# Neighbourhood attention two heads at a time, and a weight cast moved from GpSimd to ScalarE, in a three-layer kernel

## The chip, the cores and the metric

The kernel runs on one core of one Trainium2 chip. The metric is the device time of one execution in microseconds. Three runs of the kernel before gave 7265.52, 7279.33 and 7285.22, median 7279.33.

## The reference

Three layers follow one another on 2048 tokens of width 1024 with 256 context tokens. The first mixes pooling and two linear recurrences, the second a convolution and dense attention, the third a Fourier mixing and neighbourhood attention. Each has a projection in front, a gate and an output projection behind. The change touches the projection of the second layer and the neighbourhood attention of the third. In the latter the tokens form a grid of 32 rows of 64, there are 8 heads of 64, and a query sees 8 rows by 16 columns around it with a bias, and all context tokens, under one softmax:

```python
s_win = einsum('brqhd,brkwhd->bhrqkw', qg, kb) * scale + bias   # 8 rows of keys, masked to 16 columns
s_ctx = einsum('brqhd,bchd->bhrqc', qg, kc) * scale
p = softmax(concatenate([s_win, s_ctx]))
o = einsum('bhrqkw,brkwhd->brqhd', p_win, vb) + einsum('bhrqc,bchd->brqhd', p_ctx, vc)
```

## The kernel before, in words

The program is a row of stages; each stage's engines run their own lists, tied by semaphores, with a barrier between stages.

**The projection (`norm_project`, stage `p2`).** After a norm the input stands transposed in SBUF as a high and a low part (`hT`). The weights come in 22 columns of 128 (`w_sb`, two buffers). Each column is split into a high part (a cast, `split_high`, L146) and a low part (a subtraction, `split_low`, L151), both on GpSimd (L460 to L471). GpSimd may start on column n when TensorE has finished column n-2. TensorE waits for `w_split` and does for each of five token chunks (four of 512 and the context's 256) eight times three matmuls (L157 to L159). In this stage alone (`conv` is given) VectorE does the depthwise convolution of finished columns beside it: eight groups, each a few preparing instructions and then 31 taps, one SCALAR_TENSOR_TENSOR for each tap and run of tokens (L520; 60 or 90 behind one another). SyncE loads the groups' data in its own list between weight loads: group 3, for instance, in the place of column 8, behind the wait for the low part of column 6. ScalarE copies TensorE's chunks out and stores them.

**The neighbourhood attention (`neighbours`).** A first part builds the tables of biases. Then each of 8 heads goes through 16 steps of 128 queries (two grid rows). The window of a step has 9 grid rows of keys (576), the first two and last two steps have 8 (512). The 64 channels of a head are padded with zeros to 128 rows. For a step TensorE makes the scores (`win`, L2699 to L2702), VectorE adds the biases (L2772, L2775), takes the maxima (L2778 to L2780), ScalarE takes the exponentials with their sums (L2821, L2823), TensorE turns the weights by seven transposes (L2721), VectorE and ScalarE copy them to SBUF (`pt`), TensorE multiplies them with the values as the moving side (L2732), VectorE divides by the sum (L2789), TensorE turns the result (L2709), ScalarE copies it to `y`. There are two sets of score banks, and TensorE makes the scores three steps ahead. At the start of each head its values are turned (18 transposes) before the first step.

Of the kernel before, what the change touches and what calls it, by code (L numbers as in the profile page):

```python
# [161 lines left out]
def norm_project(nc, name, x_lat, x_ctx, mod, gain, w, out, groups, ident, eps, later=(), conv=None):  # L162
# [9 lines left out]
    with ExitStack() as ctx:  # L172
# [246 lines left out]
        with nc.Block() as block:  # L419
# [42 lines left out]
            def _(pool):  # L462
                for n in range(0 if later else 1, M):
# [5 lines left out]
                    split_high(nc.gpsimd, w_part[n % 2][0][:], w_sb[n % 2][:]).then_inc(w_high, 1)  # L469
# [63 lines left out]
            def _(act):  # L533
# [2031 lines left out]
def neighbours(nc, QKV, rpb, one_hot, ident, yT, row0):  # L2565
# [8 lines left out]
    VG = [range(0, 6), range(6, 12), range(12, 18)]  # L2574
    NGRP = len(VG) + 2 * QT + 1
# [7 lines left out]
    with ExitStack() as ctx:  # L2583
# [55 lines left out]

        q, k = [s.sb(f"q{u}", [P, SEQ]) for u in range(2)], [s.sb(f"k{u}", [P, T]) for u in range(2)]  # L2640
        vt = [s.sb(f"vt{u}", [HD, T]) for u in range(2)]
        v = s.sb("v", [P, NV, HD])
        NKEY = (R + 1) * ROW
        sw = [s.sb(f"sw{u}", [P, NKEY]) for u in range(2)]
        pr = [s.sb(f"p{u}", [P, NKEY + CTX]) for u in range(2)]
        pt = [s.sb(f"pt{u}", [P, 7, P]) for u in range(2)]
        mx = [s.sb(f"mx{u}", [P, 2]) for u in range(2)]
        nb = [s.sb(f"nb{u}", [P, 1]) for u in range(2)]
        sm = [s.sb(f"sm{u}", [P, 2]) for u in range(4)]
        rs = [s.sb(f"rs{u}", [P, 1]) for u in range(2)]  # L2650
        top_ = s.sb("top", [P, 1])
        o = [s.sb(f"o{u}", [P, HD]) for u in range(2)]
        y = [s.sb(f"y{u}", [HD, SEQ]) for u in range(2)]
        win = s.banks(4)
        tb = [ctx.enter_context(nc.psum_tensor(f"na_tb{u}", [P, NT], F32)) for u in range(2)]
        ob = ctx.enter_context(nc.psum_tensor("na_ob", [P, NT], F32))
        chain, zeroed = s.sem("chain"), s.sem("zeroed")
        in_full, in_used = s.sems("in_full", 2), s.sems("in_used", 2)
        s_full, s_free = s.sems("s_full", 2), s.sems("s_free", 2)
        t_full, t_free = s.sems("t_full", 2), s.sems("t_free", 2)  # L2660
        nb_ready, p_ready, pt_ready, v_ready = s.sem("nb_ready"), s.sem("p_ready"), s.sems("pt_ready", 2), s.sem("v_ready")
        o_full, o_norm, ot_out = s.sem("o_full"), s.sem("o_norm"), s.sem("ot_out")
        y_out, turn_ = s.sems("y_out", 2), s.sem("turn")

        def tiles(j):

            lo, rows, _, _ = window(j)
            n = rows * ROW
            a = [(i * P, min(P, n - i * P), lo * ROW // P + i) for i in range(-(-n // P))]
            return a + [(n + i * P, P, SEQ // P + i) for i in range(2)]  # L2670

        def heads(eng, body):
            with eng.Fori(0, NH // 2) as i:
                for u in range(2):
                    body(i * 2 + u, i, u)

        def grp(h, g):
            return g % 2, h * (NGRP // 2) + g // 2

        with nc.Block() as block:  # L2680
            @block.sync
            def _(sp):
                def body(h, pair, u):
                    sp.wait_ge(in_used[u], pair)
                    sp.dma_start(q[u][0:HD, :], QKV[ds(h * HD, HD), 0:SEQ]).then_inc(in_full[u], 16)
                    sp.dma_start(k[u][0:HD, :], QKV[ds(h * HD + NH * HD, HD), :]).then_inc(in_full[u], 16)
                    sp.dma_start(vt[u][:], QKV[ds(h * HD + 2 * NH * HD, HD), :]).then_inc(in_full[u], 16)
# [361 lines left out]
```

## Time and profile before

| | us |
|---|---|
| median of three runs | 7279.33 |
| the profiled execution | 7282.06 |
| its span | 7280.4 |
| busy in the span: TensorE matmul, weight load | 5664.7, 4331.2 |
| VectorE, ScalarE, GpSimd | 3688.1, 1714.0, 2075.9 |
| second projection, first to last matmul | 3574 to 4234 |
| attention loop, first score to last output | 6444 to 7072 |

Times in rows are counted from the span's start. The clock is the granted share of 2.4 GHz. Matmuls overlap, so a TensorE row's busy time includes the drain of its last one; the distance between starts is what it occupies.

### The profile page before, as it was taken

The numbers are of one execution on the slowest core, as the hardware profiler recorded it, in microseconds if no ns is written. First come the engines' busy times: TensorE is split into PE (matmuls) and PEld (weight loads), VectorE is DVE, ScalarE is ACT, GpSimd is POOL, SyncE is SP. The second block draws the span as 40 slices with busy tenths as digits, with TensorE's granted clock in tenths as the row PEclk, the third lists the DMA queues.
The fourth block names the chain that finished last, engine by engine and source line by source line (L and its number), as shares of the span: only waits on it lengthen the run. The fifth ranks groups of instructions, "written<-read, shape, count | busy, mean of one in ns | idle before, by whom it ended". The sixth has DMA issues, their size and how long they took to land. (4 is left out here: it accounts for less than half of the span.)

```text
span 7280.4 us, 117918 instructions
## 1 busy us (share of the span) xinstructions
PE 5664.7 (78%) x49713; PEld 4331.2 (59%) x49713; DVE 3688.1 (51%) x5261; ACT 1714.0 (24%) x3014; POOL 2075.9 (29%) x1372
## 2 busy tenths in 40 slices
PE   6899971139999556749586854999986999779989
PEld 1588850028888445627475732555574887357767
DVE  2100026654444666748499235888855000256667
ACT  2100002123332322213310021444413000124442
POOL 2211100024453312203467300766734111000002
PEclk8899985569999778879698986999996999879899
DMA  6312113332111111036322122000063211121115
GB/s 206 103 66 73 68 65 119 115 101 65 56 56 47 51 45 51 10 132 206 94 95 77 65 107 72 17 18 16 15 204 105 75 66 68 62 67 26 26 57 176
DMA packets 395963, 572.21 MB, mean 79 GB/s; under 512 B 62982, under 2 KB 296070, under 8 KB 375806
## 3 DMA queue, kind: packets, MB, share of 16 engines
q1 hardware_dynamic: 351126, 394.12, 17.4%
q10 hardware_dynamic: 33576, 127.83, 4.4%
q0 software_dynamic: 10752, 42.89, 2.1%
q8 instruction: 390, 6.39, 0.4%
q14 instruction: 119, 0.97, 0.0%
HBM read 360.86 MB, written 203.90 MB: 78 GB/s over the span
## 5 line engine op out<-in xcount | busy, mean ns | idle before, releaser
L157 PE MATMUL p_bank<-p_hT_high,p_w_high 128*128 128x512 f32 (+1 forms) x2928 | 1105.3, 377 | 139.4 <-POOL p_w_low L151 121.5
L158 PE MATMUL p_bank<-p_hT_low,p_w_high 128*128 128x512 f32 (+1 forms) x2928 | 1103.7, 377 | 0.0
L159 PE MATMUL p_bank<-p_hT_high,p_w_low 128*128 128x512 f32 (+1 forms) x2928 | 1102.7, 377 | 0.0
L491 DVE COPY p_o<-p_bank 128x512 f32<-128x512 f32 (+1 forms) x142 | 90.7, 639 | 1256.5 <-PE p_bank L159 1256.5
L146 POOL CAST p_w_high<-p_w 128x1024 fp32r<-128x1024 f32 x79 | 334.4, 4233 | 1345.7 <-issue 1152.6
L157 PEld LDWEIGHTS p_bank<-p_hT_high,p_w_high 128*128 128x128 f32 x2928 | 555.9, 190 | 242.1 <-POOL p_w_low L151 122.8
L158 PEld LDWEIGHTS p_bank<-p_hT_low,p_w_high 128*128 128x128 f32 x2928 | 555.7, 190 | 99.9
L159 PEld LDWEIGHTS p_bank<-p_hT_high,p_w_low 128*128 128x128 f32 x2928 | 555.1, 190 | 100.3
L2334 POOL TENSOR_TENSOR at_acc<-at_acc,at_p 128x512 f32<-128x512 f32 x256 | 426.4, 1665 | 142.2 <-ACT at_p L2272 120.5
L2376 DVE TENSOR_REDUCE at_mx<-at_mb 128x2 f32<-128x1024 f32 (+1 forms) x292 | 356.9, 1222 | 107.7 <-PE at_mb L2175 105.9
L1197 PE MATMUL rsc_db<-rsc_W,rsc_TK 64*64 64x64 f32 x8640 | 382.6, 219 | 4.6 <-issue 3.8
L2272 ACT ACTIVATE at_p<-at_sc 128x1024 f32<-128x1024 f32 (+1 forms) x296 | 284.9, 1013 | 400.3 <-PE at_sc L2164 348.4
L520 DVE SCALAR_TENSOR_TENSOR p_cy<-p_cu,p_wt,p_cy 128x512 f32<-128x512 f32 (+1 forms) x600 | 372.5, 700 | 0.0
L491 ACT COPY p_o<-p_bank 128x512 f32<-128x512 f32 x114 | 67.0, 588 | 1281.2 <-PE p_bank L159 1281.2
L157 PE MATMUL o_bank<-o_w_high,o_m_high 128*128 128x512 f32 x800 | 314.6, 393 | 66.9 <-POOL o_m_low L151 66.9
L1197 PEld LDWEIGHTS rsc_db<-rsc_W,rsc_TK 64*64 64x64 f32 x8640 | 355.1, 136 | 5.6 <-issue 4.5
L158 PE MATMUL o_bank<-o_w_low,o_m_high 128*128 128x512 f32 x800 | 313.4, 392 | 0.0
L159 PE MATMUL o_bank<-o_w_high,o_m_low 128*128 128x512 f32 x800 | 313.2, 391 | 0.0
L1169 POOL TENSOR_TENSOR rsc_TK<-rsc_TK,rsc_lv 128x768 f32<-128x768 f32 x108 | 195.8, 1813 | 329.4 <-DVE rsc_TK L1343 329.4
L2196 PE MATMUL at_ob<-at_p,at_V 128*64 128x512 f32 (+1 forms) x1184 | 283.3, 599 | 0.7 <-ACT at_osb L2279 0.7
L1575 DVE TENSOR_TENSOR hg_P<-hg_sc,hg_mk 128x1024 f32<-128x1024 f32 x192 | 225.8, 1218 | 110.7 <-PE hg_sc L1648 110.3
L1352 DVE TENSOR_TENSOR rsc_W<-rsc_W,rsc_db 128x512 f32<-128x512 f32 x270 | 171.1, 634 | 207.5 <-PE rsc_db L1197 205.8
(375 smaller groups left out, 11285.8 us busy)
## 6 DMA issues: line engine op xcount, KB each, us to landing
rsc_X<-rwkv_chunks SPq DMA_DIRECT2D x108, 320.0 KB, 4.5
pT<-p_o ACTq DMA_DIRECT2D x28, 1152.0 KB, 4.2
pT<-p_o ACTq DMA_DIRECT2D x29, 1024.0 KB, 3.9
o_z<-pT SPq DMA_DIRECT2D x50, 512.0 KB, 5.3
o_y<-y SPq DMA_DIRECT2D x50, 512.0 KB, 6.7
pT<-p_o ACTq DMA_DIRECT2D x88, 256.0 KB, 2.0
p_w<-in_w_in_dram SPq DMA_DIRECT2D x33, 512.0 KB, 3.9
x<-o_o ACTq DMA_DIRECT2D x32, 512.0 KB
```

The costliest lines, as they stand in the source:

```text
L146: return eng.tensor_copy(high, x)
L157: nc.tensor.matmul(out, lhs[0], rhs[0], start=start, stop=False)
L158: nc.tensor.matmul(out, lhs[0], rhs[1], start=False, stop=False)
L159: return nc.tensor.matmul(out, lhs[1], rhs[0], start=False, stop=stop)
L520: x = nc.vector.scalar_tensor_tensor(dst, src, wt[:, t, k:k + 1], dst, ALU.mult, ALU.add)
L1169: nc.gpsimd.tensor_tensor(tk[:, K_LB:K_LB + LV, d, :], tk[:, K_A:K_A + 1, d, :].broadcast_to([P, LV, P]), lv[:, d, :, :], ALU.mult).then_i ...
L1197: return nc.tensor.matmul(out, l, r, start=start, stop=stop)
L1575: nc.vector.tensor_tensor(PR[n % 2][h][:], sc[h][:], mk[:, d], ALU.mult).then_inc(sc_evac[h], 1)
L2196: m = nc.tensor.matmul(ob[h * HD:(h + 1) * HD, 0:n], V[:, tiles[j], kv * HD:(kv + 1) * HD], pr[t % 4][:, h, 0:n], start=(j == 0), stop=(t ...
L2272: nc.scalar.activation(pr[t % 4][:, :, 0:n], sc[t % 2][:, :, 0:n], ACT.Exp, scale=SC).then_inc(exp_done, 1)
L2334: nc.gpsimd.tensor_tensor(acc[b % 2][:, 1, 0:n], acc[b % 2][:, 1, 0:n], pr[t % 4][:, 1, 0:n], ALU.add).then_inc(sum_b, 1)
L2376: r = nc.vector.reduce_max(mx[b % 2][:, :, t:t + nt, c], mb[:, :, 0:nt * n].rearrange("p h (j k) -> p h j k", j=nt), AX)
```

## The change

**Weights of the second projection.** GpSimd leaves the cast out there, ScalarE makes it. ScalarE casts column 1 at the beginning, and column n+1 after it has copied the first chunk of column n.

```diff
                         pool.wait_ge(b_full[c], uses(n - 1, c))
                     pool.sem_inc(w_part_turn, 1)
-                    split_high(nc.gpsimd, w_part[n % 2][0][:], w_sb[n % 2][:]).then_inc(w_high, 1)
+                    if not conv:
+                        split_high(nc.gpsimd, w_part[n % 2][0][:], w_sb[n % 2][:]).then_inc(w_high, 1)
                     pool.wait_ge(w_high, n + 1)
                     split_low(nc.gpsimd, w_part[n % 2][1][:], w_sb[n % 2][:], w_part[n % 2][0][:]).then_inc(w_split, 1)
...
+                def cast_weights(n):
+                    act.wait_ge(w_full[n % 2], (n // 2 + 1) * 16)
+                    if n >= 2:
+                        act.wait_ge(b_full[4], n - 1)
+                    nc.scalar.copy(w_part[n % 2][0][:], w_sb[n % 2][:]).then_inc(w_high, 1)
+
+                if conv:
+                    cast_weights(1)
                 for k in range(5 * M if conv else 0):
                     n, c = divmod(k, 5)
                     cnt = CHUNKS[c][1]
+                    if c == 1 and 2 <= n + 1 < M:
+                        cast_weights(n + 1)
                     if k >= NO:
```

**Neighbourhood attention.** 64 steps for pairs of heads take the place of 128. The two heads' channels stand in rows 0 to 63 and 64 to 127 of `q` and `k` (no zeros). The scores of both go into one set of four banks, `win`. The sums, the maxima and the copies take both heads in one instruction where they can. In the product with the values the values are the stationary side (64 columns for each head) and the turned weights move, so the output comes out already turned. The inverse of the sums is spread to 64 columns for each head (`rep`) and turned by a product with the identity into the fourth quarter of `tb`; ScalarE copies it with the weights, and VectorE multiplies it in. The values of the next pair are turned within the steps 4, 6, 8, 10 and 12 of a pair. The loops over heads are written out.

```diff
+        vt = s.sb("vt", [P, T])
+        v = [s.sb(f"v{u}", [P, NV, P]) for u in range(2)]
+        sw = [s.sb(f"sw{u}", [P, 2, NKEY]) for u in range(2)]
+        pr = [s.sb(f"p{u}", [P, 2, NKEY + CTX]) for u in range(3)]
+        pt = [s.sb(f"pt{u}", [P, 2, 8, P]) for u in range(2)]
...
+        win = ctx.enter_context(nc.psum_tensor("na_win", [P, 2, 2, NT], F32))
+        ta, tb = (ctx.enter_context(nc.psum_tensor(f"na_t{n}", [P, NT], F32)) for n in "ab")
+        ob = [ctx.enter_context(nc.psum_tensor(f"na_ob{u}", [P, NT], F32)) for u in range(2)]
...
+                def scores(n):
+                    p, j = STEPS[n]
+                    a, width = lo * ROW, rows * ROW
+                    if j == 0:
+                        pe.wait_ge(qk_in[p % 2], 32 * (p // 2 + 1))
+                    if n:
+                        pe.wait_ge(added, n)
+                        pe.wait_ge(ctx_exp, 2 * n)
+                    for part, at, keys in ((0, 0, slice(a, a + NT)), (1, CTX, slice(a + NT, a + width)), (1, 0, slice(SEQ, T))):
+                        if keys.stop > keys.start:
+                            for h in range(2):
+                                r = slice(h * HD, (h + 1) * HD)
+                                m = nc.tensor.matmul(win[:, h, part, at:at + keys.stop - keys.start], q[p % 2][r, j * P:(j + 1) * P], k[p % 2][r, keys],
+                                                     start=True, stop=True)
+                    m.then_inc(s_full, 1)
+
+                def turn(n, h):
+                    p, j = STEPS[n]
+                    pe.wait_ge(win_exp, 2 * n + h + 1)
+                    pe.wait_ge(ta_out, 2 * n + h)
+                    pe.wait_ge(tb_out, 2 * n + h)
+                    for i, c, w, _ in slots(j):
+                        bank = ta if i < 4 else tb
+                        tr = nc.tensor.transpose(bank[0:w, i % 4 * P:(i % 4 + 1) * P], pr[n % 3][:, h, c:c + w], idn[:])
+                        if i == 3:
+                            tr.then_inc(ta_full, 1)
+                    if h:
+                        pe.wait_ge(rep_ready, n + 1)
+                        tr = nc.tensor.matmul(tb[:, 3 * P:4 * P], rep[:].rearrange("p h c -> p (h c)"), idn[:], start=True, stop=True)
+                    tr.then_inc(tb_full, 1)
+
+                def values(n):
+                    p, j = STEPS[n]
+                    tl = slots(j)
+                    pe.wait_ge(ta_out, 2 * n + 2)
+                    pe.wait_ge(tb_out, 2 * n + 2)
+                    if n >= 2:
+                        pe.wait_ge(o_norm, n - 1)
+                    if j == 0:
+                        pe.wait_ge(v_ready, VTILES * (p + 1))
+                    for x, (i, _, w, kt) in enumerate(tl):
+                        for h in range(2):
+                            r = slice(h * HD, (h + 1) * HD)
+                            m = nc.tensor.matmul(ob[n % 2][r, 0:P], v[p % 2][0:w, kt, r], pt[n % 2][0:w, h, i, :], start=(x == 0), stop=(x == len(tl) - 1))
...
+                for n, (p, j) in enumerate(STEPS):
+                    turn(n, 0)
+                    if n + 2 < NS:
+                        scores(n + 2)
+                    turn(n, 1)
+                    if n:
+                        values(n - 1)
+                    if j in VT_AT and p + 1 < NPAIR:
+                        pe.wait_ge(ta_out, 2 * n + 2)
+                        turn_values(p + 1, VT_AT.index(j))
+                        pe.wait_ge(v_ready, (p + 1) * VTILES + VT_AT.index(j) + 1)
+                values(NS - 1)
...
+                def add(n):
+                    p, j = STEPS[n]
                     lo, rows, d0, inner = window(j)
+                    dve.wait_ge(s_full, n + 1)
+                    if n >= 2:
+                        dve.wait_ge(win_exp, 2 * n - 2)
+                    table = bi[:, 2 * p:2 * p + 2, :, :] if inner else bt[:, 2 * p:2 * p + 2, d0:d0 + R, :]
+                    table = table.rearrange("p h d w -> p h (d w)")
+                    a = nc.vector.tensor_tensor(sw[n % 2][:, :, 0:NT], win[:, :, 0, :], table[:, :, 0:NT], ALU.add)
                     if inner:
+                        a = nc.vector.tensor_tensor(sw[n % 2][:, :, NT:NKEY], win[:, :, 1, CTX:CTX + ROW], table[:, :, NT:NKEY], ALU.add)
+                    a.then_inc(added, 1)
+                def maxima(n):
+                    p, j = STEPS[n]
+                    nc.vector.reduce_max(mx[:, :, 1], win[:, :, 1, 0:CTX], AX)
+                    dve.wait_ge(added, n + 1)
+                    nc.vector.reduce_max(mx[:, :, 0], sw[n % 2][:, :, 0:window(j)[1] * ROW], AX).then_inc(maxed, 1)
+                    dve.wait_ge(maxed, n + 1)
+                    nc.vector.reduce_max(top[:], mx[:], AX).then_inc(topped, 1)
+                    dve.wait_ge(topped, n + 1)
+                    if n >= 2:
+                        dve.wait_ge(win_exp, 2 * n - 2)
+                    nc.vector.tensor_scalar(nb[n % 2][:], top[:], -SC, None, ALU.mult).then_inc(nb_ready, 1)
+                def inverse(n):
+                    dve.wait_ge(win_exp, 2 * n + 2)
+                    nc.vector.tensor_tensor(rs[:], sm[n % 2][:, :, 0], sm[n % 2][:, :, 1], ALU.add).then_inc(summed, 1)
+                    dve.wait_ge(summed, n + 1)
+                    nc.vector.reciprocal(rs[:], rs[:]).then_inc(inverted, 1)
+                    dve.wait_ge(inverted, n + 1)
+                    if n:
+                        dve.wait_ge(tb_full, 2 * n)
+                    nc.vector.tensor_copy(rep[:], rs[:].rearrange("p (h o) -> p h o", o=1).broadcast_to([P, 2, HD])).then_inc(rep_ready, 1)
+                def take(n, h):
+                    dve.wait_ge(ta_full, 2 * n + h + 1)
+                    if n >= 2:
+                        dve.wait_ge(o_full, n - 1)
+                    nc.vector.tensor_copy(pt[n % 2][:, h, 0:4, :].rearrange("p a b -> p (a b)"), ta[:]).then_inc(ta_out, 1)
+                def scale(n):
+                    p, j = STEPS[n]
+                    dve.wait_ge(o_full, n + 1)
+                    dve.wait_ge(tb_out, 2 * n + 2)
+                    if p >= 2 and j == 0:
+                        dve.wait_ge(y_out[p % 2], 16 * (p // 2))
+                    nc.vector.tensor_tensor(y[p % 2][:, j * P:(j + 1) * P], ob[n % 2][:, 0:P], pt[n % 2][:, 1, 7, :], ALU.mult).then_inc(o_norm, 1)
...
+                for n in range(NS):
+                    take(n, 0)
+                    if n >= 2:
+                        scale(n - 2)
+                    if n + 2 < NS:
+                        add(n + 2)
+                    take(n, 1)
+                    if n + 2 < NS:
+                        maxima(n + 2)
+                    if n + 1 < NS:
+                        inverse(n + 1)
+                scale(NS - 2)
+                scale(NS - 1)
...
+                def exp_ctx(n):
+                    w = window(STEPS[n][1])[1] * ROW
+                    act.wait_ge(nb_ready, n + 1)
+                    if n >= 3:
+                        act.wait_ge(tb_full, 2 * n - 4)
+                    if n >= 2:
+                        act.wait_ge(rep_ready, n - 1)
+                    for h in range(2):
+                        nc.scalar.activation(pr[n % 3][:, h, w:w + CTX], win[:, h, 1, 0:CTX], ACT.Exp, bias=nb[n % 2][:, h:h + 1], scale=SC,
+                                             accum_out=sm[n % 2][:, h, 1:2]).then_inc(ctx_exp, 1)
+                def exp_win(n, h):
+                    w = window(STEPS[n][1])[1] * ROW
+                    nc.scalar.activation(pr[n % 3][:, h, 0:w], sw[n % 2][:, h, 0:w], ACT.Exp, bias=nb[n % 2][:, h:h + 1], scale=SC,
+                                         accum_out=sm[n % 2][:, h, 0:1]).then_inc(win_exp, 1)
+                def take(n, h):
+                    act.wait_ge(tb_full, 2 * n + h + 1)
+                    if n >= 2:
+                        act.wait_ge(o_norm if h else o_full, n - 1)
+                    w = 3 + h
+                    nc.scalar.copy(pt[n % 2][:, h, 4:4 + w, :].rearrange("p a b -> p (a b)"), tb[:, 0:w * P]).then_inc(tb_out, 1)
...
+                for n, (p, j) in enumerate(STEPS):
+                    if n + 1 < NS:
+                        exp_ctx(n + 1)
+                    for h in range(2):
+                        take(n, h)
+                        if n + 1 < NS:
+                            exp_win(n + 1, h)
+                    if j in VT_AT and p + 1 < NPAIR:
+                        keep_values(p + 1, VT_AT.index(j))
```

How the instructions stand now. ScalarE in the second projection, one column, before (`p_o` is the copied chunk, `pT` its place in memory):

```order
L538 DMA pT<-p_o 128x256
L546 ACTIVATE p_o<-p_bank 128x512
L538 DMA pT<-p_o 128x512
L546 ACTIVATE p_o<-p_bank 128x512
L538 DMA pT<-p_o 128x512
L546 ACTIVATE p_o<-p_bank 128x512
L538 DMA pT<-p_o 128x512
L546 ACTIVATE p_o<-p_bank 128x256
L538 DMA pT<-p_o 128x512
L546 ACTIVATE p_o<-p_bank 128x512
L538 DMA pT<-p_o 128x256
```

and now:

```order
L557 ACTIVATE p_o<-p_bank 128x512
L539 DMA pT<-p_o 128x256
L545 CAST p_w_high<-p_w 128x1024
L557 ACTIVATE p_o<-p_bank 128x512
L539 DMA pT<-p_o 128x512
L557 ACTIVATE p_o<-p_bank 128x512
L539 DMA pT<-p_o 128x512
L557 ACTIVATE p_o<-p_bank 128x512
L539 DMA pT<-p_o 128x512
L557 ACTIVATE p_o<-p_bank 128x256
L539 DMA pT<-p_o 128x512
L557 ACTIVATE p_o<-p_bank 128x512
```

The cast of the next column stands behind the first chunk's copy and the store of the chunk before it.

TensorE in an inner step of the attention, before (one head; `na_p` the weights, `na_o` the output of two steps back):

```order
L2721 MATMUL na_tb<-na_idn,na_p 128x128 x4
L2718 REGISTER_ALU
L2721 MATMUL na_tb<-na_idn,na_p 64x128
L2721 MATMUL na_tb<-na_idn,na_p 128x128 x2
L2709 MATMUL na_tb<-na_idn,na_o 64x128
L2699 MATMUL na_bank<-na_k,na_q 128x512
L2701 MATMUL na_bank<-na_k,na_q 128x64
L2702 MATMUL na_bank<-na_k,na_q 128x256
L2732 MATMUL na_ob<-na_v,na_pt 128x64 x7
```

and now (two heads; `x2` with `na_win` is one matmul for each head):

```order
L2728 MATMUL na_ta<-na_idn,na_p 128x128 x4
L2728 MATMUL na_tb<-na_idn,na_p 64x128
L2728 MATMUL na_tb<-na_idn,na_p 128x128 x2
L2717 MATMUL na_win<-na_k,na_q 128x512 x2
L2717 MATMUL na_win<-na_k,na_q 128x64 x2
L2717 MATMUL na_win<-na_k,na_q 128x256 x2
L2728 MATMUL na_ta<-na_idn,na_p 128x128 x4
L2728 MATMUL na_tb<-na_idn,na_p 64x128
L2728 MATMUL na_tb<-na_idn,na_p 128x128 x2
L2733 MATMUL na_tb<-na_idn,na_rep 128x128
L2748 MATMUL na_ob<-na_pt,na_v 64x128 x14
```

The scores stand between the turns of the first and the second head, two steps ahead instead of three; the product with the values is that of the step before.

VectorE in an inner step, before (one head):

```order
L2772 TENSOR_TENSOR na_sw<-na_bank,na_bi 128x512
L2775 TENSOR_TENSOR na_sw<-na_bank,na_bi 128x64
L73 REGISTER_ALU
L2778 TENSOR_REDUCE na_mx<-na_sw 128x1
L2779 TENSOR_REDUCE na_mx<-na_bank 128x1
L73 REGISTER_ALU
L2780 TENSOR_REDUCE na_top<-na_mx 128x1
L73 REGISTER_ALU
L2781 TENSOR_SCALAR na_nb<-na_top 128x1
L2782 REGISTER_ALU
L2786 TENSOR_TENSOR na_rs<-na_sm 128x1
L73 REGISTER_ALU
```

and now (two heads):

```order
L2820 COPY na_pt<-na_ta 128x512
L2828 TENSOR_TENSOR na_y<-na_ob,na_pt 128x128
L2789 TENSOR_TENSOR na_sw<-na_win,na_bi 128x2x512
L2791 TENSOR_TENSOR na_sw<-na_win,na_bi 128x2x64
L2820 COPY na_pt<-na_ta 128x512
L2796 TENSOR_REDUCE na_mx<-na_win 128x2
L2798 TENSOR_REDUCE na_mx<-na_sw 128x2
L2800 TENSOR_REDUCE na_top<-na_mx 128x2
L2804 TENSOR_SCALAR na_nb<-na_top 128x2
L2808 TENSOR_TENSOR na_rs<-na_sm 128x2
L2810 RECIPROCAL na_rs<-na_rs 128x2
L2814 COPY na_rep<-na_rs 128x128
```

The second copy of turned weights (`na_ta`) stands between the add and the maxima of the same scores.

## Rows read from the trace of the kernel before

**Rows 1.** Busy time by engine in four stretches; then clock, DMA share, GB/s.

```profile
2600.00:2800.00 200.00, 114.27 (x1672) 98.13 (x1672) 130.72 (x147) 63.65 (x48) 69.97 (x56) 0.80 0.11 44
3574.00:4234.00 660.00, 555.99 (x2640) 468.99 (x2640) 416.78 (x644) 61.99 (x110) 330.20 (x42) 0.91 0.24 77
...
6444.00:7072.00 628.00, 577.32 (x3552) 459.40 (x3550) 432.89 (x1248) 276.49 (x889) 3.78 (x7) 0.92 0.10 25
```

**Rows 2.** Timeline of TensorE, one attention step: start, busy, line, tiles, shape, count.

```profile
6561.64 1.02 PE L2699 MATMUL na_bank<-na_k,na_q 128*128 128x512 f32 x2
...
6563.15 1.95 PE L2732 MATMUL na_ob<-na_v,na_pt 128*128 128x64 f32 x14
6564.94 0.93 PE L2721 MATMUL na_tb<-na_idn,na_p 128*128 128x128 f32 x7
...
6565.82 0.59 PE L2699 MATMUL na_bank<-na_k,na_q 128*128 128x512 f32 x1
```

**Rows 3.** Timeline of GpSimd, second projection, late columns.

```profile
4111.07 1.04 POOL L146 CAST p_w_high<-p_w 128x1024 fp32r<-128x1024 f32 x1 [21.15 <-issue]
4112.19 2.39 POOL L151 TENSOR_TENSOR p_w_low<-p_w,p_w_high 128x1024 fp32r<-128x1024 f32 x1
4135.73 1.04 POOL L146 CAST p_w_high<-p_w 128x1024 fp32r<-128x1024 f32 x1 [21.15 <-issue]
```

**Rows 4.** Waits, 3560 to 4250: who waited for whom, total us, times, longest.

```profile
PE p_bank L157 <- POOL p_w_low L151: 103.2, 5, 28.9
```

**Rows 5.** Timeline of GpSimd, second projection, two early stretches.

```profile
3651.02 30.60 POOL L146 CAST p_w_high<-p_w 128x1024 fp32r<-128x1024 f32 x1 [21.15 <-issue]
...
3684.86 1.23 POOL L146 CAST p_w_high<-p_w 128x1024 fp32r<-128x1024 f32 x1
...
3796.82 50.01 POOL L146 CAST p_w_high<-p_w 128x1024 fp32r<-128x1024 f32 x1 [4.22 <-issue]
```

**Rows 6.** Timeline of VectorE in the same stretches.

```profile
3640.89 39.83 DVE L520 SCALAR_TENSOR_TENSOR p_cy<-p_cu,p_wt,p_cy 128x512 f32<-128x512 f32 x60
...
3794.22 51.71 DVE L520 SCALAR_TENSOR_TENSOR p_cy<-p_cu,p_wt,p_cy 128x512 f32<-128x512 f32 x90
```

**Rows 7.** Tile o_w_high: ScalarE's casts, ns min/median/max, first and last start.

```profile
L637 ACT CAST o_w_high<-o_w x24: 1044/1046/1057, 3279.1 to 7099.3; 128x1024 fp32r<-128x1024 f32 x24
```

**Rows 8.** Timelines of VectorE and GpSimd, first output projection.

```profile
3280.17 7.62 DVE L151 TENSOR_TENSOR o_w_low<-o_w,o_w_high 128x1024 fp32r<-128x1024 f32 x4
...
3280.28 2.01 POOL L146 CAST o_m_high<-o_m 128x1024 fp32r<-128x1024 f32 x1 [161.78 <-DVE o_m L695]
3282.37 3.20 POOL L151 TENSOR_TENSOR o_m_low<-o_m,o_m_high 128x1024 fp32r<-128x1024 f32 x1
...
3304.00 1.23 DVE L708 SCALAR_TENSOR_TENSOR o_r<-o_x,o_r 128x1024 f32<-128x1024 f32 x1
...
3304.08 3.42 POOL L151 TENSOR_TENSOR o_m_low<-o_m,o_m_high 128x1024 fp32r<-128x1024 f32 x1
```

**Rows 9.** Tile p_cg, second projection: its loads, from issue to landing.

```profile
DMA to landing us min/median/max: 4.6/5.7/8.1
```

**Rows 10.** Timeline of TensorE, dense attention: products with 64-column stationaries.

```profile
4702.22 1.94 PE L2196 MATMUL at_ob<-at_p,at_V 128*64 128x512 f32 x8
```

**Rows 11.** Groups of the page: busy us, mean ns, idle before.

```profile
L2376 DVE TENSOR_REDUCE at_mx<-at_mb 128x2 f32<-128x1024 f32 (+1 forms) x292 | 356.9, 1222 | 107.7 <-PE at_mb L2175 105.9
...
L1575 DVE TENSOR_TENSOR hg_P<-hg_sc,hg_mk 128x1024 f32<-128x1024 f32 x192 | 225.8, 1218 | 110.7 <-PE hg_sc L1648 110.3
```

**Rows 12.** Groups by shape in the attention loop, 6444 to 7072.

```profile
L2795 DVE COPY na_pt<-na_tb 128x512 f32<-128x512 f32 x128 | 87.4, 682 | 5.6 <-PE na_tb L2721 3.8
...
L2821 ACT ACTIVATE na_p<-na_bank,na_nb 128x256 f32<-128x256 f32 x128 | 60.7, 474 | 74.1 <-DVE na_nb L2781 55.1 <-ACT na_y L2829 17.5 <-ACT na_pt L2843 1.5
L2779 DVE TENSOR_REDUCE na_mx<-na_bank 128x1 f32<-128x256 f32 x128 | 52.9, 413 | 0.0
...
L2821 ACT ACTIVATION_READ_ACCUMULATOR na_p<-na_bank,na_nb 128x1 f32 x128 | 24.7, 193 | 0.0
```

More of the change, by code:

```diff
@@ L2573, in neighbours @@
     NV = T // P
-    VG = [range(0, 6), range(6, 12), range(12, 18)]
-    NGRP = len(VG) + 2 * QT + 1
     def window(j):
@@ L2645, in neighbours @@
[L2645 to L2661, printed above, removed]
@@ L2667, in tiles, with slots @@
+        def slots(j):
             lo, rows, _, _ = window(j)
             n = rows * ROW
[L2669 to L2678, printed above, removed]
+            a = [(i, i * P, min(P, n - i * P), lo * ROW // P + i) for i in range(-(-n // P))]
+            return a + [(5 + i, n + i * P, P, SEQ // P + i) for i in range(2)]
@@ L2680, in neighbours, with groups @@
+        def groups(t):
+            return range(4 * t, min(4 * t + 4, NV))
         with nc.Block() as block:
@@ new lines, in turn_values @@
+                def turn_values(p, t):
+                    if t == 0:
+                        pe.wait_ge(v_in, 16 * (p + 1))
+                    if p * VTILES + t:
+                        pe.wait_ge(v_ready, p * VTILES + t)
+                    for x, kt in enumerate(groups(t)):
+                        tr = nc.tensor.transpose(ta[:, x * P:(x + 1) * P], vt[:, kt * P:(kt + 1) * P], idn[:])
+                    tr.then_inc(v_turned, 1)
+                pe.wait_ge(zeroed, 1)
+                scores(0)
@@ new lines, in _ @@
+                for t in range(VTILES):
+                    turn_values(0, t)
+                scores(1)
+                pe.wait_ge(v_ready, VTILES)
+                for n, (p, j) in enumerate(STEPS):
[9 more added lines that the diff above has]
+                        pe.wait_ge(v_ready, (p + 1) * VTILES + VT_AT.index(j) + 1)
@@ new lines, in _ @@
+                nc.vector.memset(tb[:], 0.0).then_inc(zeroed, 1)
+                add(0)
+                maxima(0)
+                add(1)
+                maxima(1)
+                inverse(0)
+                for n in range(NS):
[9 more added lines that the diff above has]
+                        inverse(n + 1)
@@ new lines, in keep_values @@
+                def keep_values(p, t):
+                    act.wait_ge(v_turned, p * VTILES + t + 1)
+                    if p >= 2 and t == 0:
+                        act.wait_ge(o_full, QT * (p - 1))
+                    g = groups(t)
+                    nc.scalar.copy(v[p % 2][:, g[0]:g[-1] + 1, :].rearrange("p a b -> p (a b)"), ta[:, 0:len(g) * P]).then_inc(v_ready, 1)
+                for t in range(VTILES):
+                    keep_values(0, t)
+                exp_ctx(0)
+                exp_win(0, 0)
@@ L2879, in _ @@
                 for u in range(2):
[L2880 to L2889 removed]
+                    pool.wait_ge(y_out[u], 16 * NPAIR // 2)
```

206 lines of the change are left out of this document (31 added, 175 removed).

## The prediction

> **What bounds the kernel now.** I read the stretches first, because the chain that ended last names only the tail. Two stretches are touched. The second projection runs from 3574 to 4234 us and the loop of the neighbourhood attention from 6444 to 7072 us [rows 1]. The reader should see that TensorE is the bound in both: busy 556 of 660 us and 577 of 628 us. The profiled execution took 7282.06 us around a span of 7280.4, against a median of 7279.33; my sum starts at 7282, and under 0.3% (22 us) could not be told from no change.
>
> In the attention loop one inner step of one head takes TensorE 4.18 us at full clock [rows 2]: scores 1.51 (6561.64 to 6563.15), values 1.79 (to 6564.94), eight transposes 0.88 (to 6565.82, where the next scores start). Nothing else is near it. Over 628 us for 128 steps it is 4.9 us a step, the rest being each head's start and stretches at 1.2 GHz.
>
> In the projection a column (one 128-wide slice of the weights, 120 matmuls) takes 24.66 us: the undisturbed casts on GpSimd are that far apart [rows 3]. The waits show 103.2 us in five pieces in which TensorE stood still for GpSimd's low part of the weights [rows 4]. The timeline of GpSimd says why: a cast of 1.04 us took 30.60 and 50.01 us [rows 5], both times until the end of an unbroken run of VectorE's convolution taps (SCALAR_TENSOR_TENSOR x60 from 3640.89 for 39.83 us, x90 from 3794.22 for 51.71 us) [rows 6]. There are eight such runs, from 3641 to 4056. Behind the cast, in the same gap between runs, GpSimd also gets the low part and the next column's cast (3684.86) [rows 5] and low part done. So each gap feeds up to two columns.
>
> **The change in the projection.** The cast leaves GpSimd for ScalarE. It costs ScalarE 1.05 us a column [rows 7], and ScalarE is busy 62 of 660 us [rows 1]: hidden. What stays on GpSimd is the low part, a TENSOR_TENSOR that reads SBUF just as the cast did. Does it also wait for a run of taps? A single instruction shows that it is exposed: o_m_low took 3.42 us, where a low part takes 2.39 [rows 3], when a SCALAR_TENSOR_TENSOR had started 0.08 us before it [rows 8]. No row shows a low part arriving inside a run. The nearest other row speaks for less: among VectorE's TENSOR_TENSORs (o_w_low x4 from 3280.17) a GpSimd low part got in after one of them, 3.20 us long. But the cast also waited for only one there (2.01 us) [rows 8] and still sat through 88 taps in the projection. The two GpSimd operations behave alike against one partner, so I take it that they do against the other: the low part takes over the cast's wait. The bounds of this term are the 103 us given back whole, and the worst walk below.
>
> The Trainium skill ("SBUF — State Buffer", section "Who interferes with whom") says that a VectorE instruction with two SBUF inputs and a GpSimd instruction that reads SBUF exclude each other, and that the one that comes second waits for the whole instruction. The trace agrees that they exclude each other (3.42 against 2.39 us) and differs on the length: 50 us is a run of instructions, not one. By the page's rule the low part would wait under 1 us; that is the first rival.
>
> With the wait kept, the order now hurts. ScalarE casts column n+1 only after it has copied the first chunk of column n, whereas GpSimd could do two columns in one gap. The low part of n+1 can start no earlier than the chunk (24.66 / 4.5 = 5.4 us), its copy (taken as 0.7, as VectorE's 512-wide copy [rows 12]), the cast (1.05) and handovers after the start of column n: some 7.5 us, near 10 after a stop, since TensorE restarts at 1.2 GHz. The gap between runs is some 4 us. So each gap feeds one column. The walk, with 2.4 us for a low part:
> Column 4: waits for run 1 to end, 3681; TensorE stops 10 us. Column 5: its low part comes near 3694, run 2 has begun, it waits until 3738; stop 30 us. Column 6: run 3 ends near 3784; stop 19 us. Group 3's data is asked for by SyncE only once the low part of column 6 is done, and lands 5.7 us after issue [rows 9]; VectorE stands idle and column 7's low part slips through. The same repeats: columns 8, 9 stop 13 and 19 us, 10 passes, 11 and 12 stop 13 and 27, 13 passes, 14 stops 13. The last run ends near 4077 instead of 4056, still covered by TensorE. Stops: 10 + 30 + 19 + 13 + 19 + 13 + 27 + 13 = 144 us in eight pieces, against 103 in five. Each restart costs about 2 us: the clock of 0.91 over 660 us is some 119 us at 1.2 GHz, 103 of them idle, the rest half lost over five restarts. Sum: 144 - 103 + 6 = +47 us. Columns 7, 10 and 13 pass with about 2 us to spare; each that misses adds up to 30, hence +100 at worst.
>
> **The change in the attention.** Two heads a step, 64 steps. TensorE per double step: scores of both heads on the two 64-row halves, 1.51 us if they run side by side; 14 transposes at 0.11, 1.54; the small product 0.22 (as two 128-column instructions); values with 64-column stationaries. For these there is a row: at_ob, 128*64, eight 512-column instructions in 1.94 us [rows 10], 0.24 each where a 512-column one of the scores takes 0.43 (1.02 for two with the drain [rows 2]); so two run at a time. The 28 instructions of 128 columns are then a quarter of 0.24 each: 1.7. A change of tile shape costs about 0.12: of the 1.79 us of values 14 x 0.11 are work, the rest is the 64-row tile in their midst. Four a step, 0.5. Together 5.4 us where two single steps took 8.36. Half-row scores are the unseen part; bounded by 1.51 (side by side) and 3.02.
>
> But TensorE stops being the bound. There is now one set of score banks. The loop through it: ScalarE's two context exponentials, 2 x 0.47 + 0.19 = 1.13 [rows 12]; scores 1.51 + 0.2 + 0.16 to drain = 1.87; VectorE's add of 2x512, 1.22 by the 1024-wide form [rows 11], and of 2x64, 0.2; the second take of `ta`, 0.60 net [rows 12]; maxima 0.68 (256 wide takes 0.413 [rows 12]), 1.36 (1024 wide takes 1.22 [rows 11]) and two short ones of 0.15 (estimate), 2.35 with overlaps; handovers 0.15. Sum 7.5 us, for the 16 edge steps 7.1: 48 x 7.5 + 16 x 7.1 = 474 us. Adding the first take, scale and inverse, VectorE is busy 6.0 us of it, ScalarE 3.4; TensorE idles a piece of over 2 us in each step. What is hidden: transposes, values and the value turns of the next pair (5 groups of 0.4 us) sit in TensorE's idle time, ScalarE's window exponentials beside the scores.
>
> The clock then matters. At 92% busy the loop has 0.92 granted; the stretch 2600 to 2800 with TensorE 57% busy has 0.80 [rows 1]. At 5.4 of 7.5 (72%) I read 0.87, a quarter of the time at 1.2 GHz. There TensorE needs 10.8 us a step and binds. Mean step: 1 / (0.74/7.4 + 0.26/10.8) = 8.06 us, 516 us in all. The start adds 7 us (a pair's values are 1.2 MB and are turned before the first product; bounds 0 to 15). 523 against 628: -105 us. Bounds: -237 (VectorE alone, 6.0 a step) and +70 (10.8 throughout); I stay near the loop sum, all of whose terms but one have rows.
>
> **Sum.** 7282 - 105 + 47 = 7224 us. Own range of this case 7165 to 7280.
>
> **Rivals.**
> 1. The low part is not held by a run of taps (the page's rule, or a difference between cast and TENSOR_TENSOR). For: o_m_low got in after one instruction. Against: so did the cast, and it was starved all the same. Then the 103 us go: 7282 - 105 - 103 = 7074.
> 2. The clock holds the attention at 1.2 GHz, and it ends slower. Place: the attention loop; price: TensorE's 5.4 us become 10.8. For: every step has one idle piece over 2 us, and 57% busy already cost 20% of the clock. Against: at 1.2 GHz TensorE is fully busy, and in the loop of now the clock comes back from such stretches (0.92 over the whole). It decides from a mean step of (628 - 47 - 7) / 64 = 9.0 us on; at 10.8 throughout 7282 + 70 + 47 = 7399.
> 3. The half-row scores run one after the other. Against: at_ob shows column halves side by side. Then the loop is 9.0 us, 583 in all: 7282 - 45 + 47 = 7284, no change: the second half of the change would not do what it says.
>
> **How the numbers follow.** My forecast 67%, rival 1 17%, rival 2 8%, rival 3 8%. Forecast 7224. The range is 7060 to 7300: it takes in most of rival 1 and the no-change case, and leaves out rival 2 and the lower part of rival 1 with a fast loop, below 2 in 10. Faster by over 0.3%: 0.65 of my case and rival 1, 0.82. Within: rival 3 and the worst walk, 0.10. Slower: rival 2, 0.08.
>
> **What would show it.** In the projection: no CAST on GpSimd, p_w_low instructions of 15 to 50 us, TensorE waiting about 144 us for p_w_low in eight pieces, the stage near 707 us instead of 660. If p_w_low stays under 4 us and the stage takes 557, rival 1 is right. In the attention: a loop of 500 to 530 us; TensorE about 72% busy with its first score matmul of each step released by ScalarE's context exponential, VectorE's add released by the scores; a clock near 0.87. Score matmuls of shape 64*128 with equal or staggered starts show rows 64 to 127 beside rows 0 to 63; a clock near 0.6 shows rival 2. The forecast is wrong if either stage differs from its figure by over 50 us, or if any other stage moves by more than a few us.

## The result and the profile after

The changed kernel takes 7170.84 us (median of four runs, 7167.77 to 7174.35) against 7279.68 for the kernel before (also four runs): ratio 0.9854, 95% interval 0.9836 to 0.9871. That is 109 us less where 55 were forecast (7224). The profiled execution has a span of 7172.6 us.

First the two stretches that [rows 1] show of before, now 3574 to 4281 and 6484 to 6966 us (same columns: busy by engine, clock, DMA share, GB/s):

```profile
3574.00:4281.00 707.00, 563.64 (x2640) 473.91 (x2640) 401.18 (x644) 82.75 (x134) 313.24 (x24) 0.89 0.22 72
6484.00:6966.00 482.00, 389.07 (x3496) 279.99 (x3492) 345.38 (x751) 236.45 (x661) 1.64 (x3) 0.95 0.08 29
```

From first to last matmul the projection went from 659.4 to 701.3 us (+42, forecast +47) and the attention from 629.3 to 482.6 (-147, forecast -105). Every other stage of TensorE kept its length within 5 us. The two edits pull in opposite directions, and the median shows only their sum.

**The projection.** The waits of that stretch, answering [rows 4], have more and not less for the low part:

```profile
PE p_bank L157 <- POOL p_w_low L151: 137.7, 8, 31.8
```

GpSimd's timeline, answering [rows 5], has no cast, and the low part stands where the cast stood:

```profile
3662.32 25.18 POOL L151 TENSOR_TENSOR p_w_low<-p_w,p_w_high 128x1024 fp32r<-128x1024 f32 x1 [22.27 <-ACT p_w_high L545]
3697.15 47.04 POOL L151 TENSOR_TENSOR p_w_low<-p_w,p_w_high 128x1024 fp32r<-128x1024 f32 x1 [9.65 <-ACT p_w_high L545]
3754.46 33.87 POOL L151 TENSOR_TENSOR p_w_low<-p_w,p_w_high 128x1024 fp32r<-128x1024 f32 x1 [10.27 <-ACT p_w_high L545]
3798.70 3.07 POOL L151 TENSOR_TENSOR p_w_low<-p_w,p_w_high 128x1024 fp32r<-128x1024 f32 x1 [10.37 <-ACT p_w_high L545]
```

VectorE's timeline answers [rows 6]:

```profile
3690.28 51.71 DVE L521 SCALAR_TENSOR_TENSOR p_cy<-p_cu,p_wt,p_cy 128x512 f32<-128x512 f32 x90
...
3746.30 39.83 DVE L521 SCALAR_TENSOR_TENSOR p_cy<-p_cu,p_wt,p_cy 128x512 f32<-128x512 f32 x60
3786.09 0.10 DVE L503 MEMSET p_cu<- 128x30 f32 x2
3798.27 3.78 DVE L509 TENSOR_TENSOR p_cu<-p_cu,p_cg 128x1039 f32<-128x1039 f32 x2 [12.07 <-DMA p_cg<-pT]
```

The low part that arrives at 3697.15, 7 us into the run from 3690.28, ends at 3744.19, 2.2 us behind the run's end (3690.28 + 51.71 = 3741.99). The next one, held by the next run, ends at 3788.33. The fourth passes: VectorE is then waiting 12.07 us for the data of group 3, as the walk had it. ScalarE's timeline shows why only one column passes in a gap:

```profile
3695.53 0.60 ACT L557 ACTIVATE p_o<-p_bank 128x512 f32<-128x512 f32 x1 [15.26 <-PE p_bank L159]
...
3696.03 1.04 ACT L545 CAST p_w_high<-p_w 128x1024 fp32r<-128x1024 f32 x1
```

The cast of column 5 begins only at 3696.03, behind the chunk of column 4, 5.75 us into the new run.

**The attention.** TensorE's timeline of one inner double step at full clock answers [rows 2]:

```profile
6704.20 1.78 PE L2717 MATMUL na_win<-na_k,na_q 64*128 64x512 f32 x12 [0.15 <-ACT na_p L2860]
6705.91 0.66 PE L2728 MATMUL na_ta<-na_idn,na_p 128*128 128x128 f32 x4
6706.40 0.49 PE L2728 MATMUL na_tb<-na_idn,na_p 128*64 128x128 f32 x3
6706.73 0.39 PE L2733 MATMUL na_tb<-na_idn,na_rep 128*128 128x128 f32 x2
6707.05 2.05 PE L2748 MATMUL na_ob<-na_pt,na_v 128*64 128x128 f32 x28
6709.03 0.66 PE L2728 MATMUL na_ta<-na_idn,na_p 128*128 128x128 f32 x4
6709.52 0.49 PE L2728 MATMUL na_tb<-na_idn,na_p 128*64 128x128 f32 x3
6711.49 1.09 PE L2717 MATMUL na_win<-na_k,na_q 64*128 64x512 f32 x3 [1.48 <-ACT na_p L2860]
```

Scores of both heads take 1.71 us (6704.20 to 6705.91), hardly more than one head's 1.51: they run side by side. With two sets of transposes (0.82 and 0.82), the product 0.32 and the values 1.98, TensorE works 5.65 us. Yet the next scores start 7.29 us after the last, released by ScalarE's exponential. What sets the distance is a ring of waits through the one set of score banks: the scores wait for the context exponentials of the step before, these for the maxima, the maxima for the add, and the add for its scores. The waits of the loop name two links of it:

```profile
PE na_win L2717 <- ACT na_p L2860: 76.3, 54, 3.1
...
DVE na_sw L2789 <- PE na_win L2717: 127.6, 64, 10.9
```

### The profile page after: what moved, and what is told of

Read it like the earlier page. It is cut to its first block and busy times, and to the rows that moved or that the text cites. A ratio compares the mean times of both kernels' runs of the same rounds, so it can differ in the third digit from the quotient of the medians.

```text
span 7172.6 us, 115094 instructions
## 1 busy us (share of the span) xinstructions
PE 5483.4 (76%) x49641; PEld 4149.3 (58%) x49641; DVE 3597.3 (50%) x4766; ACT 1691.4 (24%) x2804; POOL 2044.9 (29%) x1343
## 5 line engine op out<-in xcount | busy, mean ns | idle before, releaser
L151 POOL TENSOR_TENSOR p_w_low<-p_w,p_w_high 128x1024 fp32r<-128x1024 f32 x79 | 448.3, 5675 | 358.0 <-ACT p_w_high L545 353.4
L146 POOL CAST p_w_high<-p_w 128x1024 fp32r<-128x1024 f32 x58 | 60.3, 1039 | 1062.5 <-issue 1011.8
```

The costliest lines, as they stand in the source:

```text
L151: return eng.tensor_tensor(low, x, high.bitcast(F32), ALU.subtract)
```

## Experiments

Times are medians; each ratio is to runs of the kernel before on the same chip.

**Each edit alone.** The first kernel is the one before with `cast_weights`, its calls and `if not conv:` added; the second is the changed one without them.

> The kernel before with the cast of the second projection's weights on ScalarE and nothing else changed. My theory: GpSimd's low part is held by a run of convolution taps as its cast was, and because ScalarE casts column n+1 only after the first chunk of column n, a gap between runs feeds one column instead of two. The changed kernel's projection took 701.3 us against 659.4, so this kernel should take 7280 + 42 = 7322 us, TensorE waiting 138 us for p_w_low in eight pieces and the attention unchanged at 629. Rival A: the longer projection comes of the other edit (another SBUF layout, other timing): 7280 us and 103 us of waits. Rival B: the change of the attention alone accounts for more or less than its stage shows, by work that runs across the barrier: then this and the run with the attention alone do not add up to -109.

> The changed kernel with the cast of the second projection's weights back on GpSimd. My theory: projection 659 us as before, attention 483 us as in the changed kernel, total 7280 - 147 = 7133 us, 38 us faster than the changed kernel. Rival A (the projection is slower for another reason than the cast): 7171 us. Rival B (GpSimd's work has nothing to do with it, TensorE's clock does): between the two.

The cast alone: 7331.13, ratio 1.0057 (1.0040 to 1.0074); the projection took 700.5 us, TensorE waited 138.6 us for `p_w_low` in 8 pieces. The heads alone: 7127.71, ratio 0.9785 (0.9769 to 0.9801); projection 659.0, attention 478.7. Against their own runs of the kernel before the two make +42 and -161 us, together -119 where both at once gave -109; the intervals are some 12 us to each side, so the sum does not tell more. The stages do: 700.5 and 659.0 are the projections of the changed kernel and of the one before within 1 us, and the attention differs by 4 us from the changed kernel's and, with the cast alone, by 6 us (635.4) from that of before. So neither edit is needed for what the other does, and the cast's move, in this place of ScalarE's list, is a loss.

**The cast earlier in ScalarE's order.**

```diff
-                    if c == 1 and 2 <= n + 1 < M:
+                    if c == 0 and 2 <= n + 1 < M:
```

> The changed kernel, but ScalarE casts column n+1 before the first chunk of column n is copied instead of after it. Both theories agree that GpSimd's low part is held by the runs of taps; they differ on what made it worse than before. Order theory (mine): the cast of n+1 is then done when TensorE stands still, so a gap between runs again feeds two columns, with 1 us less of GpSimd's work in it: about five stops and 100 us of waits, projection near 655 us, total near 7125. Rival (the low part by itself is held longer than the cast was, whatever the order): still eight stops, 138 us, 7171.

7118.95, ratio 0.9768 (0.9751 to 0.9784); projection 651.1. A gap feeds two columns again (two low parts in one row), and five stops are left:

```profile
3660.27 33.80 POOL L151 TENSOR_TENSOR p_w_low<-p_w,p_w_high 128x1024 fp32r<-128x1024 f32 x2 [22.27 <-ACT p_w_high L545]
```
```profile
PE p_bank L157 <- POOL p_w_low L151: 95.3, 5, 27.1
```

So the order theory holds: the extra 42 us came from the place of the cast in ScalarE's list, one chunk too late, and not from the low part being held worse than the cast.

**Breaking the run of taps.** A pause (the tap waits for the one right before it, and no longer only for the last tap on its own tokens, which is two or three instructions back), or a clear of 8 columns of a spare tile:

```diff
-                                dve.wait_ge(tap_done, TAPS[i] + (k - 1) * len(RUNS[half]) + r + 1)
+                                done = TAPS[i] + k * len(RUNS[half])
+                                dve.wait_ge(tap_done, done if k % 8 == 0 and r == 0 else done - len(RUNS[half]) + r + 1)
```

```diff
                             x.then_inc(tap_done, 1)
+                        if k % 8 == 7:
+                            nc.vector.memset(filler[:], 0.0)
```

> The changed kernel, but every eighth tap of the convolution waits for the tap right before it, so that VectorE drains and its unbroken run has a short pause in it about every 6 to 8 taps' time. Theory P: it is the lack of any gap that keeps GpSimd out; a pause of even 0.1 us lets the waiting low part in. Then no p_w_low takes over about 16 us (24 taps of 0.66), TensorE never stops in the projection, which takes about 563 to 570 us: total near 7035. Theory Q: GpSimd only gets in where the kind of VectorE's instruction changes (the ends of runs, where it got in before): no change but the pauses, 240 of about 0.1 us beside other work, 7171.

> The changed kernel with a clear of 8 columns of a spare tile (MEMSET, no wait of its own) behind every eighth tap of the convolution. The pause of the run before let GpSimd in; this asks whether it was the pause or merely that something other than a tap stood there, as at the ends of the runs. Theory D (the drained engine lets GpSimd in): the MEMSETs overlap their neighbours without a gap, so nothing changes: eight stops, 138 us, 7171. Theory K (another kind of instruction lets it in, since in the kernel before GpSimd got in beside a MEMSET and a TENSOR_TENSOR without any pause): as with the pauses, at most one stop of about 20 us, 7030.

With pauses 7028.43, ratio 0.9642 (0.9626 to 0.9658); with clears 7034.59, ratio 0.9671 (0.9653 to 0.9689). Each projection takes 567 us. Theory P was right on the pause. Theory D fell with the clear: VectorE need not stand still, a MEMSET between two taps is enough. (Eight groups with three breaks each make 24, not the 240 of the expectation.) GpSimd's low parts with pauses, and then VectorE and GpSimd with clears:

```profile
3658.07 5.06 POOL L151 TENSOR_TENSOR p_w_low<-p_w,p_w_high 128x1024 fp32r<-128x1024 f32 x1 [22.27 <-ACT p_w_high L546]
...
3707.39 8.95 POOL L151 TENSOR_TENSOR p_w_low<-p_w,p_w_high 128x1024 fp32r<-128x1024 f32 x1 [22.11 <-ACT p_w_high L546]
```
```profile
3654.81 8.20 DVE L522 SCALAR_TENSOR_TENSOR p_cy<-p_cu,p_wt,p_cy 128x512 f32<-128x512 f32 x9
3660.15 0.07 DVE L525 MEMSET p_filler<- 128x8 f32 x1
3662.93 2.73 DVE L522 SCALAR_TENSOR_TENSOR p_cy<-p_cu,p_wt,p_cy 128x512 f32<-128x512 f32 x4
```
```profile
3657.52 4.94 POOL L151 TENSOR_TENSOR p_w_low<-p_w,p_w_high 128x1024 fp32r<-128x1024 f32 x1 [22.27 <-ACT p_w_high L548]
```

The low part is issued at 3657.52 in the middle of the taps and ends at 3662.46, about its own 2.4 us behind the MEMSET at 3660.15. The tap there lasts until 3663.01, from 3660.13: now VectorE waits for GpSimd.

The Trainium skill ("SBUF — State Buffer", section "Who interferes with whom") says that who issues first holds the shared ports for the whole instruction. That GpSimd and a tap exclude each other the trace bears out; but a low part that took 47.04 us was held by a run of taps and not by one. One reading would be that the following tap, which starts some 0.08 us before the last one ends, takes the ports over before GpSimd can. It does not fit the VectorE TENSOR_TENSORs that let GpSimd in, in the kernel before:

```profile
3281.45 1.92 DVE L151 TENSOR_TENSOR o_w_low<-o_w,o_w_high 128x1024 fp32r<-128x1024 f32 x1
3283.29 3.36 DVE L151 TENSOR_TENSOR o_w_low<-o_w,o_w_high 128x1024 fp32r<-128x1024 f32 x1
```

The second starts at 3283.29, 0.08 us before the end of the first (3281.45 + 1.92 = 3283.37), just as a tap does, and yet the low part that had been waiting since 3282.37 went first and ended at 3285.57. So an early start of the next instruction is not enough to keep GpSimd out. That the unbroken run of taps holds it and that a break ends this is shown; why is open.

**The last stop.** With pauses TensorE still stood 20.5 us once.

```diff
-            GROUPS_AT = {4: (0, 1), 6: (2,), 8: (3,), 9: (4,), 11: (5,), 13: (6,), 14: (7,)}
+            GROUPS_AT = {4: (0, 1), 6: (2,), 8: (3,), 9: (4,), 11: (5,), 13: (6,), 16: (7,)}
```

> The run with a pause every eighth tap, and SyncE asks for the last convolution group's data in the place of column 16 instead of 14. With the pauses TensorE still stood 20.5 us for column 15: its weights were queued on SyncE behind that group, which waits for VectorE. If that is the cause the stop goes and the projection takes about 546 us, total 7028 - 20 = 7008. Rival (the low part of column 15 was late for GpSimd's sake, or the stop moves to another column): 7028.

7021.80, ratio 0.9642 (0.9628 to 0.9657). The projection takes 544.5 us without a stop. The interval does not set the total apart from that of the pauses alone, whose ratio was the same against another set of runs; the stage does, 566.8 to 544.5. SyncE's timeline with pauses alone shows the cause, the weights of column 15 behind the group's transfers:

```profile
3899.07 0.45 SPq L446 DMA_DIRECT2D p_w<-in_ab_w_in_dram  x1
3953.58 0.80 SPq L440 DMA_DIRECT2D y<-p_cy  x2
...
3956.72 23.70 SPq L446 DMA_DIRECT2D p_w<-in_ab_w_in_dram  x4
```

**What bounds the attention's step.** First the scores' wait split (with the order of `win`'s banks and the two counts of `s_full` changed to match):

```diff
                     if n:
                         pe.wait_ge(added, n)
-                        pe.wait_ge(ctx_exp, 2 * n)
                     for part, at, keys in (...):
+                        if at == CTX:
+                            m.then_inc(s_full, 1)
+                            if n:
+                                pe.wait_ge(ctx_exp, 2 * n)
```

> The changed kernel, but the 512-wide scores of a step wait only for VectorE's add, and only the 64- and 256-wide ones for ScalarE's context exponentials; VectorE's 512-wide add waits only for the former. No work is added or left out. Loop theory (mine): the step of 7.29 us is the chain exponentials 1.16, scores 1.82, VectorE from the add to the negated maximum 4.3; with 1.0 us of the scores and the hand-over out of it VectorE's own 5.9 us become the bound, TensorE's 5.65 just under it. A step of about 6.0 us (edges 5.6) gives 48 x 6.0 + 16 x 5.6 + 25 for start and clock = 403 us against 483: total 7091. Rival T (TensorE's work and its clock set the step): no change, 7171.

Then more and less work for TensorE, the product of the inverses six times, and the values' product with `tl[:4]`:

```diff
+                        for _ in range(6):
                             tr = nc.tensor.matmul(tb[:, 3 * P:4 * P], rep[:].rearrange("p h c -> p (h c)"), idn[:], start=True, stop=True)
```

```diff
-                    for x, (i, _, w, kt) in enumerate(tl):
+                    for x, (i, _, w, kt) in enumerate(tl[:4]):
```

> The changed kernel with the small product of the inverses done six times over instead of once (same result), 1.1 us more of TensorE's work in each of the 64 steps. Loop theory: TensorE stands idle 1.64 us of a step of 7.29, so the work is hidden and the clock falls less often: 7171, or up to 10 us less. Rival T (TensorE sets the step): 64 x 1.1 = 70 us more, 7241. In between if the later turned inverse (ScalarE's second copy waits for it) lands on the loop.

> The changed kernel with only the first four of the seven key tiles multiplied with the values; the last three are left out, 0.85 us less of TensorE's work in a step. Rival T: 64 x 0.85 = 54 us less, 7117. Loop theory: nothing gained. Clock rule of the forecast (the granted clock follows the mean busy share: 4.8 of 7.29 is 66%, for which it would give about 0.84): time is lost, about 20 us more than 7171 with the granted clock of the loop down from 0.95. If the clock stays at 0.95 the rule was wrong also in direction: 7171.

Split: 7084.42, ratio 0.9735 (0.9717 to 0.9754); attention 396.1 us, most inner steps 5.74 us, 7.08 where values are turned. The ring was the bound. In an inner step of the split kernel TensorE goes from the scores (2.09 us) to transposes, product and values without a gap and VectorE is busy nearly throughout; which of the two bounds it now the run does not tell. (The order of `win`'s banks changed in the same run and was not tested by itself.) More work: 7181.07, ratio 0.9877 (0.9859 to 0.9896), attention 491.3; most steps keep their 7.29 or 6.74. The 15 steps with value turns grew, 12 of them to 8.29 and the three at an edge to 7.64. There 5.65 + 1.1 us and the turn (7.08 against 5.74 in the split kernel, 1.34 us) come to 8.1, more than the ring. The expectation had overlooked them. Less work (the products with the last three of the seven key tiles are left out): 7182.13, ratio 0.9873 (0.9856 to 0.9890), attention 496.2: 0.85 us a step taken from TensorE made the stage 14 us longer. The loop of the kernel with more and of the one with less:

```profile
6484.00:6966.00 482.00, 438.26 (x4063) 337.08 (x4064) 345.44 (x748) 234.34 (x659) 1.65 (x3) 0.99 0.07 25
```
```profile
6484.00:6966.00 482.00, 351.82 (x2694) 251.60 (x2696) 337.61 (x735) 229.46 (x647) 1.64 (x3) 0.89 0.07 26
```

The granted clock was 0.99 and 0.89 around the changed kernel's 0.95. Two inner steps of the changed kernel show what this does:

```profile
6644.44:6653.14 8.70, 7.45 (x56) 5.06 (x57) 5.46 (x13) 3.50 (x11) 0.00 (x0) 0.80 0.01 2
6689.61:6696.90 7.29, 5.82 (x56) 4.22 (x57) 5.78 (x14) 3.65 (x11) 0.00 (x0) 1.00 0.00 0
```

In the long step VectorE and ScalarE are not busy for longer. TensorE, which for part of it runs at 1.2 GHz (half of full speed; mean 0.80), is busy 1.63 us longer with the same 56 instructions, and the ring waits for it. In the kernel with less work such steps of 7.8 to 9.3 us come 17 times instead of 6. Of the outcomes set down for it, the one by the forecast's reading of the clock had the direction: it gave about 20 us more at 0.84, where the stage took 14 us more at 0.89.

**All together, and the cast's place again.** Pauses, the later group and the split scores; then the same with the cast back on GpSimd.

> The three edits together: pause every eighth tap, last group later, and the 512-wide scores not waiting for the context exponentials; the cast stays on ScalarE. The stages stand apart behind barriers, so the gains should add: 7171 - 143 (pauses) - 20 (group) - 87 (scores) = 6921.

> The kernel of the run before, with the weights' cast of the second projection back on GpSimd: with pauses GpSimd gets in for the cast and again for the low part. Theory: each of the two now waits at most a pause's distance (8 to 16 us with 2 or 3 taps a step), so cast and low part together mostly fit into the 24.66 us of a column, and where the cast runs has next to no price: 6921 to 6940. Rival (the move to ScalarE is worth its place as soon as GpSimd is let in at all, since two waits in a row miss the column): stops of up to 10 us in several columns, 6950 to 7000.

6922.35, ratio 0.9503 (0.9490 to 0.9516), and 6923.22, ratio 0.9511 (0.9495 to 0.9527). The gains add: projection 544.6, attention 394.6. Once GpSimd is let in, no difference shows between the two places of the cast; with it on GpSimd TensorE waits 1.1 us once.

## Why the prediction was right or wrong

The total lies in the stated range, but that range (7060 to 7300) would have taken in rival 1 at 7074 as well, and of the case's own range (7165 to 7280) 7171 is near the lower end. What bears the forecast out or not is the two stages.

**The low part takes over the cast's wait: right.** The eight low parts that were held took 20 to 49 us; TensorE stood 137.7 us in eight pieces for the 144 in eight forecast. Rival 1 (not held, 7074) is out. It rested on the rule of the Trainium skill, and on one row in which GpSimd got in among VectorE's TENSOR_TENSORs; why those let it in and the taps don't stays open, since no run put TENSOR_TENSORs in the taps' place. (The cast of before sat through 85 taps that started behind it, not 88; nothing hangs on that.)

**One column a gap: right,** and shown by the run with the earlier cast, in which a gap feeds two. The walk named columns 4, 5, 6, 8, 9, 11, 12 and 14; the stops came before 4, 5, 6, 8, 9, 11, 13 and 14, of 7.8, 29.6, 16.4, 16.5, 16.7, 16.4, 2.5 and 31.8 us. At the end the walk is off by a column: the third wait of VectorE for a group's data inside the loop of groups, 10.28 us, let column 12 pass (its low part took 2.39 us at 3980.05) and not 13, so 27 us forecast there became none, and the 13 before column 14 became 31.8. That these cancel in the sum is luck. The stage grew by 42 instead of 47: 34.5 of waits and 7.4 around three more restarts, 2.5 each where 2 were taken.

**TensorE's work in a step of the attention: right within 5%.** 5.65 us for 5.4. The score halves run side by side, so rival 3 is out. The values took 1.98 us where 1.7 and a share of the 0.5 for changes of tile shape stood.

**The ring as the bound: right,** 7.29 us for 7.5, edges 6.74 for 7.1: 48 x 7.29 + 16 x 6.74 = 458 for 474. The trace of the step gives exponentials 1.16, scores 1.82, add 1.34, take 0.60, maxima 2.37 where 1.13, 1.87, 1.42, 0.60 and 2.35 stood; the 0.15 us set apart for handovers is within them.

**The clock: the step that failed.** "At 5.4 of 7.5 (72%) I read 0.87, a quarter of the time at 1.2 GHz" put 42 us on it. The loop was granted 0.95, and the steps above their full-clock length sum to 9.8 us. This term alone is 32 of the 40 us missed; the ring gives 16 more, and start and end took 15 where 7 stood. The reading took the clock as following the mean busy share of a stretch from another stage. The rows do not bear it out: 577 of 628 us busy had 0.92 in the kernel before, 389 of 482 had 0.95 in the changed one, and 438 of 482, the same 91 to 92% as before, had 0.99 in the one with more work. That TensorE was busy 81% and not 72% explains little of it: a straight line between the two rows that the forecast used gives 0.85 at 72% and 0.88 at 81%. Nor did a step at the lower level take the 10.8 us of the forecast: after the first two steps the slowest took 8.87. Within one loop the direction is right (0.89, 0.95, 0.99 with rising work), the size was not to be had from a mean. Rival 2 (1.2 GHz throughout, 7399) did not come about. What in the step's pattern makes one step fall and the next not was not settled.

**The sum.** 7282 + 42 - 147 = 7177, with the other stages' few us the 7174 of the profiled execution. The projection's error (5 us, from stops of the wrong size) and the attention's (40 us, mostly the clock) had no common cause.

## What to carry to other kernels

Where GpSimd is kept out by an unbroken run of VectorE's SCALAR_TENSOR_TENSORs, moving one of its instructions away only hands the wait to the next; break the run (a wait on the last tap, or one tiny MEMSET, every eighth tap), and place what feeds the held engine before, not behind, the work of the column under way. When a loop's bound is a ring through one set of banks, ask for each wait in it which banks it protects: splitting one wait gave 87 us, while work taken from the engine that idles gave less than nothing. Profile each of two edits by its stage: one of them may be hiding a loss.

## What the runs showed that was not expected

A clear of 0.07 us without any wait opened the run of taps as well as a pause did. There are only three such places in each convolution group of 31 taps, and the entry shown made one tap 2.1 us longer. And less work for TensorE (351.82 busy us for 389.07) made the same loop 14 us longer, at a granted clock of 0.89 for 0.95; this had been one of three outcomes set down, and neither theory of what bounds the loop gave it.
